# Fourier token transform on half its columns, rope tables on Pool, waits per norm tile, ropes beside qz

## What is computed

```python
def rms_norm(x, g):
    xf = x.astype(jnp.float32)
    y = xf * lax.rsqrt(jnp.mean(xf * xf, axis=-1, keepdims=True) + NORM_EPS)
    return (y * g.astype(jnp.float32)).astype(x.dtype)

def fourier_mix(h, w_in, w_out):
    b, n, _ = h.shape
    u, z = jnp.split(h @ w_in, 2, axis=-1)
    ug = u.reshape(b, n, FOURIER_GROUPS, D_BRANCH // FOURIER_GROUPS).astype(jnp.float32)
    mixed = jnp.fft.fft2(ug, axes=(1, 3), norm='ortho').real
    y = mixed.reshape(b, n, D_BRANCH).astype(h.dtype) * jax.nn.silu(z)
    return y @ w_out

def window_attention_mix(h, hc, w_in, sink, w_out, cos, sin, with_ctx_out):
    q, k, v, z = split_qkvz(h, w_in)
    qc, kc, vc, zc = split_qkvz(hc, w_in)
    q = apply_rope(q, cos, sin) * ATTN_SCALE
    k = apply_rope(k, cos, sin)
    ...
    out = (o * jax.nn.silu(z)) @ w_out
```

## Time and profile before

| | us |
|---|---|
| median of the runs | 3273.3 |
| lowest, highest | 3270.9, 3274.6 |
| profiled execution, its own time | 3273.4 |
| its span, first to last instruction | 3271.6 |
| PE busy | 3098.4 (95%) |
| DVE busy | 2398.7 (73%) |
| ACT busy | 1374.0 (42%) |
| POOL busy | 272.9 (8%) |

### The profile page before, as it was taken

How to read it: one execution, slowest core, us unless ns; L and a number is a source line. 1 busy time by engine, 2 the same in 40 slices (tenths; PEclk the granted TensorE clock), 3 DMA queues, 4 the chain that set the end, 5 groups by cost and what they waited for, 6 DMA issues and landing times.

```text
span 3271.6 us, 58750 instructions
## 1 busy us (share of the span) xinstructions
PE 3098.4 (95%) x24402; PEld 2958.1 (90%) x24402; DVE 2398.7 (73%) x3270; ACT 1374.0 (42%) x1470; POOL 272.9 (8%) x530
## 2 busy tenths in 40 slices
PE   5999989989999899999999999998999999899998
PEld 5997889989978799999999998996688999799998
DVE  6877888978778878865675667667867975567464
ACT  4335553443345534533433345334734333434332
POOL 0100000000000000000000110110000422000000
PEclk9999999999999999999999999999999999899999
DMA  5774456757745567665767674883156765377553
GB/s 206 278 281 170 173 172 244 275 209 279 270 167 174 201 246 255 210 237 193 256 234 257 230 267 167 295 295 142 59 215 229 225 199 189 135 263 248 194 216 129
DMA packets 130945, 710.37 MB, mean 217 GB/s; under 512 B 16392, under 2 KB 16544, under 8 KB 71584
## 3 DMA queue, kind: packets, MB, share of 16 engines
q1 hardware_dynamic: 67392, 484.47, 41.7%
q0 software_dynamic: 61264, 214.93, 18.6%
q10 hardware_dynamic: 2064, 7.70, 0.6%
HBM read 700.26 MB, written 2.10 MB: 215 GB/s over the span
## 4 chain that ended last, share of the span: by engine, by line
PE 82%; DVE 10%; ACT 4%; issue 3%; DMA 2%; ACTq 0%; DVEq 0%; POOLq 0%
PE bank L520 24%; PE bank L516 22%; PE bank L517 22%; PE bank L615 2%; DVE wlo L1594 2%; ACT whi L1044 2%; PE bank L865 1%; PE bank L844 1%; DMA aslab<-w_ada_dram 1%; DVE aslab L1619 1%; PE bank L567 1%; PE bank L625 1%; DVE sc L1713 1%; PE bank L952 1%; DVE xs L2205 1%
## 5 line engine op out<-in xcount | busy, mean ns | idle before, releaser
L516 PE MATMUL bank<-uhi,whi 128*128 128x256 f32 x6720 | 1662.0, 287 | 66.9 <-issue 35.1
L517 PE MATMUL bank<-ulo,whi 128*128 128x256 f32 x6720 | 1647.8, 285 | 0.0
L1044 ACT CAST whi<-raw 128x2048 fp32r<-128x2048 f32 (+1 forms) x464 | 876.0, 1889 | 1554.1 <-PE bank L520 1498.1
L1594 DVE TENSOR_TENSOR wlo<-raw,whi 128x2048 fp32r<-128x2048 f32 (+1 forms) x464 | 1053.4, 2271 | 614.4 <-ACT whi L1044 613.2
L516 PEld LDWEIGHTS bank<-uhi,whi 128*128 128x128 f32 x6720 | 1302.7, 194 | 76.6 <-issue 57.2
L517 PEld LDWEIGHTS bank<-ulo,whi 128*128 128x128 f32 x6720 | 1303.0, 194 | 1.2
L520 PE MATMUL bank<-uhi,wlo 128*128 128x256 f32 x6720 | 883.0, 284 | 5.5 <-DVE wlo L1594 5.5
L520 PEld LDWEIGHTS bank<-uhi,wlo 128*128 128x128 f32 x6720 | 838.6, 192 | 9.6 <-DVE wlo L1594 6.9
L460 POOL DMA_DIRECT2D aslab<-w_ada_dram x384 | 202.8, 528 | 2738.2 <-DVE mod L1619 1440.8
L1619 DVE CUSTOM_DVE_ANT_0 aslab<-aslab,sil,part 128x1024 f32<-128x1024 f32 x192 | 245.2, 1280 | 39.6 <-DMA aslab<-w_ada_dram 39.5
L1619 DVE CUSTOM_DVE_ANT_0 aslab<-aslab,sil,cols 128x1024 f32<-128x1024 f32 x192 | 245.1, 1280 | 35.4 <-DMA aslab<-w_ada_dram 35.4
(11 more groups left out here) (268 smaller groups left out, 2394.0 us busy)
## 6 DMA issues: line engine op xcount, KB each, us to landing
aslab<-w_ada_dram POOLq DMA_DIRECT2D x384, 512.0 KB, 5.0
raw<-w_win_dram SPq DMA_DIRECT2D x96, 1024.0 KB, 4.9
raw<-w_wfi_dram SPq DMA_DIRECT2D x96, 1024.0 KB, 5.3
raw<-w_wfo_dram SPq DMA_DIRECT2D x48, 1024.0 KB, 4.9
raw<-w_wci_dram SPq DMA_DIRECT2D x48, 1024.0 KB, 5.3
raw<-w_wo_dram SPq DMA_DIRECT2D x32, 1024.0 KB, 5.6
raw<-w_wpg_dram SPq DMA_DIRECT2D x32, 1024.0 KB, 5.3
raw<-w_wqz_dram SPq DMA_DIRECT2D x32, 1024.0 KB, 4.8
```

The lines of the kernel that those rows point to most:

```text
L516: nc.tensor.matmul(o, w_, xhi_, start=start, stop=False, skip_group_check=True)
L517: nc.tensor.matmul(o, w_, xlo_, start=False, stop=False, skip_group_check=True)
L1044: nc.scalar.copy(whi[:, s % 2, 0:n], raw[:, s, 0:n]).then_inc(s_hi, 1)
L1594: v.tensor_tensor(wlo[:, s, 0:n], raw[:, s, 0:n], whi[:, s % 2, 0:n].bitcast(F32), ALU.subtract).then_inc(s_lo, 1)
```

## The change

Four parts. The token transform computes columns 0 to 128 of the even and odd parts and `combine` writes the other 127 from the same columns read backwards, with the sign of the odd part turned. The rope table angles are computed on Pool, behind its first loads, with an operation more per step (Pool's multiply and add are two); ACT's Exp and Sin calls and DVE's lambda operations move inside run in0. In the first group of a run behind a norm PE waits for each tile of ulo instead of each four, and DVE's split of slab 1 moves from tile 5 of the norm to tile 8. The ropes of the second attention move behind the slabs of qz's last four groups on PE and beside their splits on DVE, and Silu of the gates into the drains.

```diff
+HALF = T // 2 + 1
@@ build @@
-        red = sb("red", 3 * T, at=place["trn"] + 3 * T * 4)
+        red = [sb(f"red{i}", 3 * T, at=place["trn"] + 3 * T * 4 * (i + 1)) for i in range(2)]
+        turns = sb("turns", 3 * T, at=place["trn"] + 3 * T * 4 * 3)
@@ gpsimd, behind load(0, 0), load(1, 1), wait for x, cond(0) @@
+            def follow(ins):
+                done[0] += 1
+                ins.then_inc(s_ang, 1)
+                pool.wait_ge(s_ang, done[0])
+            pool.wait_ge(s_in, 16 * INPUT_DMAS)
+            follow(nc.gpsimd.tensor_copy(ang[:, 0:T], posi[:, :]))
...
+            for i, (turn, back) in enumerate(((0.25, math.pi / 2), (0.0, 0.0))):
+                x = red[i][:, :]
+                follow(nc.gpsimd.tensor_scalar(trn[:, :], ang[:, :], 1 / TWO_PI, turn, ALU.mult, ALU.add))
+                follow(nc.gpsimd.tensor_scalar(trn[:, :], trn[:, :], ROUND, None, ALU.add))
+                follow(nc.gpsimd.tensor_scalar(trn[:, :], trn[:, :], -ROUND, None, ALU.add))
+                for c, y in ((C1, ang[:, :]), (C2, x), (C3, x)):
+                    follow(nc.gpsimd.tensor_scalar(turns[:, :], trn[:, :], -c, None, ALU.mult))
+                    follow(nc.gpsimd.tensor_tensor(x, turns[:, :], y, ALU.add))
+                follow(nc.gpsimd.tensor_scalar(x, x, back, PI32, ALU.add, ALU.min))
+                nc.gpsimd.tensor_scalar(x, x, -PI32, None, ALU.max).then_inc(s_sin, 1)
@@ tensor @@
-            def slab_t(s, par, lows):
+            def slab_t(s, par, lows, ready=None):
                 for k in range(4):
                     kt = 4 * s + k
+                    if ready is not None:
+                        pe.wait_ge(*ready(kt))
...
+                    if fill in NORMS and slab is slab_t:
+                        pe.wait_ge(s_hi, (g + r["m0"]) * SLABS + (s + 1))
+                        slab(s, par, False, lambda kt: (s_nl, 16 * U_NORMS[fill] + kt + 1))
...
-                            last = nc.tensor.matmul(bank[7][:, T * odd:T * (odd + 1)],
+                            last = nc.tensor.matmul(bank[7][:, T * odd:T * odd + HALF],
                                                     ab[:, g, t, P * odd:P * (odd + 1)],
-                                                    dft[:, t, T * odd:T * (odd + 1)],
+                                                    dft[:, t, T * odd:T * odd + HALF],
...
-            project("qz", None)
-            pe.wait_ge(s_drain, 2 * (RUN["qz"]["e0"] + 8))
-            for i in range(NJX):
-                rope(rope_jobs_x(), 2 * NJ, i)
+            project("qz", None, n=4)
+            def rope_behind(q):
+                if q == 2:
+                    pe.wait_ge(s_drain, 2 * (r["e0"] + 4))
+                if q < NJX:
+                    rope(rope_jobs_x(), 2 * NJ, q)
+            for g in range(4, 8):
+                group(r, g, (r["e0"] + g) % 2, slab_t, None, lambda s, g=g: rope_behind(4 * (g - 4) + s))
             pe.wait_ge(s_ro, 2 * NJ + NJX)
@@ scalar @@
+                    then=(f"v{l}",), hooks=((0, lambda: silu(2 * l)),)
+                    + (() if l else ((2, lambda_exps), (4, rope_tables))))
...
-                    nc.scalar.copy(evens[:, g % 2, :], bank[7][:, 0:T]).then_inc(s_fe, 1)
+                    nc.scalar.copy(evens[:, g % 2, 0:HALF], bank[7][:, 0:HALF]).then_inc(s_fe, 1)
...
-            act.wait_ge(s_drain, 2 * (RUN["qz"]["e0"] + 8))
-            nc.scalar.activation(zq_t[:, 16 * T:32 * T], zq_t[:, 16 * T:32 * T], ACT.Silu)\
-                .then_inc(s_gate, 1)
+            run(RUN["qz"], copier(zq_half), 0, 4, then=("qz", 4))
+            run(RUN["qz"], copier(zq_half, ACT.Silu), 4, 4)
@@ vector @@
-                    if kt == 5:
+                    if kt == 8:
                         split(RUN[AFTER_NORM[name]], 0, 1)
...
-                    v.tensor_tensor(zf[:, 2 * g, :], evens[:, g % 2, :], bank[7][:, T:2 * T], ALU.subtract)
-                    v.tensor_tensor(zf[0:P - 1, 2 * g + 1, :], evens[0:P - 1, g % 2, :],
-                                    bank[7][0:P - 1, T:2 * T], ALU.add).then_inc(s_fb, 1)
+                    even, odd = evens[:, g % 2, 0:HALF], bank[7][:, T:T + HALF]
+                    y, mirror = zf[:, 2 * g, :], zf[0:P - 1, 2 * g + 1, :]
+                    v.tensor_tensor(y[:, 0:HALF], even, odd, ALU.subtract)
+                    v.tensor_tensor(mirror[:, 0:HALF], even[0:P - 1, :], odd[0:P - 1, :], ALU.add)
+                    v.tensor_tensor(y[:, HALF:T], even[:, P - 1:0:-1], odd[:, P - 1:0:-1], ALU.add)
+                    v.tensor_tensor(mirror[:, HALF:T], even[0:P - 1, P - 1:0:-1], odd[0:P - 1, P - 1:0:-1],
+                                    ALU.subtract).then_inc(s_fb, 1)
...
-            run(RUN["qz"], nothing)
-            dve.wait_ge(s_drain, 2 * (RUN["qz"]["e0"] + 8))
+            run(r, nothing, 0, 4, then=("qz", 4))
+            def at_slab(q):
+                if q < 14:
+                    split(r, 4 + (q + 2) // 4, (q + 2) % 4)
+                ada(r, 16 + q)
+            ropes(rope_jobs_x(), 2 * NJ, table, 0, tuple((q, lambda q=q: at_slab(q)) for q in range(NJX)))
+            for q in range(NJX, 16):
+                at_slab(q)
+            dve.wait_ge(s_drain, 2 * (r["e0"] + 8))
```

More of the change, by code:

```diff
@@ L355, in build @@
         s_sin = sem("table_angle_ready")
+        s_ang = sem("table_steps")
         s_tab = sem("tables_ready")
@@ L473, in _ @@
             cond(0)
+            done = [0]
+            def follow(ins):
[4 more added lines that the diff above has]
+            follow(nc.gpsimd.tensor_copy(ang[:, 0:T], posi[:, :]))
+            for k in (2, 1, 0):
+                last = nc.gpsimd.tensor_scalar(ang[:, T * k:T * (k + 1)], ang[:, 0:T],
+                                               kk[:, K_INVF + k:K_INVF + k + 1], None, ALU.mult)
+            follow(last)
+            TWO_PI = 2 * math.pi
+            C1 = 6.28125
+            C2 = float(np.float32(np.round((TWO_PI - C1) * 2 ** 20) / 2 ** 20))
+            C3 = TWO_PI - C1 - C2
+            ROUND = 12582912.0
+            PI32 = 3.1415925
+            for i, (turn, back) in enumerate(((0.25, math.pi / 2), (0.0, 0.0))):
[8 more added lines that the diff above has]
+                nc.gpsimd.tensor_scalar(x, x, -PI32, None, ALU.max).then_inc(s_sin, 1)
             at = 2
@@ L1218, in silu, with lambda_exps, rope_tables @@
                 nc.scalar.activation(x, x, ACT.Silu).then_inc(s_sil, 1)
-            act.wait_ge(s_lam, 1)
-            act.dma_start(praw[:, :, :], vec["p"][0]).then_inc(s_p, 16)
-            nc.scalar.activation(sm[:, SM_TMP + 4:SM_TMP + 8], sm[:, SM_TMP:SM_TMP + 4], ACT.Exp)\
-                .then_inc(s_lam, 1)
-            for i in range(2):
-                act.wait_ge(s_sin, i + 1)
-                nc.scalar.activation(tabs[:, i::2, :], red[:, :].rearrange("p (k n) -> p k n", n=T),
-                                     ACT.Sin).then_inc(s_tab, 1)
+            def lambda_exps():
+                act.wait_ge(s_lam, 1)
+                act.dma_start(praw[:, :, :], vec["p"][0]).then_inc(s_p, 16)
+                nc.scalar.activation(sm[:, SM_TMP + 4:SM_TMP + 8], sm[:, SM_TMP:SM_TMP + 4], ACT.Exp)\
+                    .then_inc(s_lam, 1)
+            def rope_tables():
+                for i in range(2):
+                    act.wait_ge(s_sin, i + 1)
+                    nc.scalar.activation(tabs[:, i::2, :], red[i][:, :].rearrange("p (k n) -> p k n", n=T),
+                                         ACT.Sin).then_inc(s_tab, 1)
             def first_block(l):
@@ L1860, in _, with lambda_products @@
-            dve.wait_ge(s_tab, 2)
+            def lambda_products():
+                lv = lamr[:, :].rearrange("p (l q n) -> p l q n", l=2, q=4)
+                lp = sq[:, 0:256].rearrange("p (l q n) -> p l q n", l=2, q=2)
+                for l in range(2):
+                    last = v.tensor_tensor(lp[:, l], lv[:, l, 0:4:2], lv[:, l, 1:4:2], ALU.mult)
+                link(last)
+                v.tensor_reduce(sm[:, SM_TMP:SM_TMP + 4], sq[:, 0:256].rearrange("p (a n) -> p a n", n=64),
+                                AX.X, ALU.add).then_inc(s_lam, 1)
@@ new lines, in lambda_values @@
+            def lambda_values():
+                dve.wait_ge(s_lam, 2)
+                for l in range(2):
+                    a = SM_TMP + 4 + 2 * l
+                    link(v.tensor_tensor(sm[:, SM_LAM + l:SM_LAM + l + 1], sm[:, a + 1:a + 2], sm[:, a:a + 1],
+                                         ALU.subtract))
+                    v.tensor_scalar(sm[:, SM_LAM + l:SM_LAM + l + 1], sm[:, SM_LAM + l:SM_LAM + l + 1],
+                                    -LAM_INIT[l], None, ALU.add)
+                    link(v.tensor_scalar(sm[:, SM_SUBG + l:SM_SUBG + l + 1], col("subln_g", l),
+                                         1.0 - LAM_INIT[l], None, ALU.mult))
@@ L1881, in first_block @@
                 norm(f"n{l}")
-                run(RUN[f"in{l}"], nothing, then=(f"v{l}",))
+                run(RUN[f"in{l}"], nothing, then=(f"v{l}",),
```

(6 more changed lines are left out.)

60 lines of the change are left out of this document (9 added, 51 removed).

## The result

The median of the changed kernel is 3248.4 us (3247.7 to 3249.1, four runs), beside 3272.9 for the kernel before on the same chip: ratio 0.9928, 95% interval 0.9916 to 0.994. That is 24.5 us less where 44.2 were forecast, and outside the range of 3221 to 3242. The profiled execution's span is 3247.0, against 3271.6.

The account below looks back on a forecast made before the run. PE, busy 95% of the span, was taken as the bound. Gains 19.7 + 6.7 + 6.5 + 14.8 = 47.7, less 3.5 for Pool beside DVE, 44.2: 3273.4 - 44.2 = 3229.2 us, range 3221 to 3242.

Parts of the forecast that it names:

- The start (B): Program start: with the rope tables on Pool, the first whi begins at 18.3 instead of 25.01; 6.7 us earlier.
- C: Per-tile waits behind norms: first product earlier by 2.2 us at n0 and n1, 2.1 at nf3, nothing at nci; 6.5 us.
- Pool's chain: Rope tables on Pool, from 19.0 us: ending between 35.3 (DVE's durations) and 53 (twice the long ones), loads not held up.
- a rival priced at 4 us per operation: Rival 4: slow Pool arithmetic makes ada loads late, slower than before; 3295 us at 5 us each; chance 0.02.
- Turn-taking: Pool's arithmetic beside DVE in n0 delays the norm by 4.1 us, 0.6 of it free; cost 3.5 us.
- Rival 1: Pool and DVE take turns in full in n0, DVE 15 us late; gain 33.3 us, time 3240; chance 0.24.
- Late loads: First block: the third ada load, queued behind Pool's tables, goes out at about 57, not held up; no cost.
- A: Token transforms in three Fourier layers: 129 instead of 256 columns saves 0.82 us, 24 times; 19.7 us.
- Rivals 2 and 3: 2: weight loads bind the short transform products, 3244, chance 0.05. 3: DVE binds qz's second half, 3236, chance 0.08.
- D: Second attention's ropes moved into qz's second half: first score operation 13.8 us earlier, plus 1.0 for the clock; 14.8 us.
- Waits for late loads elsewhere: PE waiting for late condition-vector loads beyond the first block; the prediction had no term for it.

Follow-up runs that it names:

- spread_tables: Changed kernel with four long Pool table operations ahead, each other step behind one condition-vector load, ACT's Sin calls in in0's group 6, not 4; 3233.4 us, again 3231.9.
- no_tables: Changed kernel with the rope tables computed by DVE again, ahead of the program; token transform, per-tile waits and moved ropes stay; 3240.1 us, ratio 0.9906.
- first_table: Changed kernel with Pool computing the first table (cosines) in full and only one clamping operation for the second; 3240.0 us, ratio 0.9909.
- waits_only: Kernel before with only the per-tile waits of a norm's first slab and the second split behind tile 8; 3270.0 us, ratio 0.999, ten runs.
- second_after_norm: Changed kernel with one clamping operation for the first table, then Pool's full second table after the first norm, in front of the loads; 3242.8 us, ratio 0.9915.
- spread_defer: spread_tables with qz's last three condition-vector steps moved into the second attention, whose own steps go behind its fifth round; 3231.3 us, ratio 0.9885.

## Why the prediction was wrong

- **The start (B), 6.7.** The mechanism was right. The first whi came at 19.10, not 18.3, since ACT's table load of 1.28 us now stands in front of it. With most of Pool's work out of the way the first three slabs are 8.4 to 8.9 us ahead (spread_tables), against 8.9 for B and n0's part of C in the sum. Against no_tables, which has all but B, spread_tables is 6.6 us below in the medians (the intervals touch) and 5.6 by slabs at 480.
- **Pool's chain: the step that failed.** "The floor is DVE's own durations" and "The other end is twice that for the long ones", so a chain that ends between 35 and 53, and "Either end is before that, so the loads are not held up". Pool's operations took 2.13 us alone, 3.8 times DVE's, and 2.6 on average over all 22; the chain ended at 80.6. Twice DVE was no bound, only a guess in the form of one: no row had Pool's arithmetic, and then the other end has to be found by asking what length would hurt. I had that number, the third load out by about 60, a chain of 41 us, and gave it only to a rival priced at 4 us per operation with a chance of 0.02. That rival's mechanism is half of what happened; it needed 1.8 us per operation to begin. (The Trainium skill's figure, GPSIMD Engine Reference, Elementwise, made an estimate of 1.7 us for two sources; 1.80 to 2.05 were measured.)
- **Turn-taking, 3.5.** The Trainium skill's rule (SBUF — State Buffer, Who interferes with whom), that such a DVE instruction and a GpSimd instruction lock each other out for a whole one, agrees with this trace beside Pool's two-source operations: 0.41 against 2.03 us for one subtraction. Beside its one-source operations it does not hold for the whole of Pool's: 1.04 us, and DVE goes on at its usual pace while Pool's operation of 2.18 us still runs. The term was mis-sized: the norm was late by 6.8 instead of 4.1 us (two operations longer by 1.6 us, six by 0.6), and with the wait for slab 2's whi and the lower clock behind it PE lost 7.9 us (from -7.3 to +0.5). Rival 1 named this at 33.3 us for the whole change; first_table, which has this price and not the other, is 28.8 us below before.
- **Late loads, 0 in the sum.** Another 6.8 us from 61.5 to 90.3. Together the first 90 us give +7.3 where the sum had -5.4: 12.7 of the 19.7 us that are missing.
- **A, 19.7.** Right: 20.0. Rivals 2 and 3 did not happen; the reversed reads of the combine take 0.28 us like the forward ones, not twice as long.
- **C, 6.5.** n1's gap is 2.1 us shorter, as forecast; nci's gain is mostly given back, as forecast (0.5 remain in waits_only); nf3's was counted at 2.1 and keeps 0.9 in waits_only and 0.2 to 1.9 in the others, but for second_after_norm, which loses 1.6 there. I had looked for the next late thing one slab ahead only. The part alone is worth 1.2 us in time (0 to 6).
- **D, 14.8.** 13.8 by slabs in the changed kernel and 13.4 in the runs of the part alone. In the trace a condition-vector step that I did not list stands in front of the first score, behind a wait of 4.17 us; that it is the missing 1.0 us is not shown, since the runs could not tell the version that moves it (spread_defer, 0.6 us) from the one beside it.
- **Waits for late loads elsewhere**, 0 in the sum: some 7 us net in the changed kernel's profiled execution (between 90 and 2150 us, A and n1 taken out), 4 in its repetition, 2 in both traces of the spread version, and 4 to 8 in the traces of the other versions that have A and C together. The sum took the execution of before as if every other had the same waits. How much of this is chance is not settled, and what makes a load late at 626 in both traces of the changed kernel stays open.

The parts alone add up to about -26 (-20.6, -13.4, -1.2 and +9.1), against -24.5 measured together: within what the runs can tell, no dependence among them shows.

## What to carry to other kernels

Moving arithmetic to an idle engine is free only if its queue holds nothing else that is due: price the chain from a row of that engine, and where there is none, work out from which length it would hold up what is queued behind it, and give that case a real chance. The same work cost 13 us here in front of the loads and nothing that the runs can tell between them. A gap made shorter in front of a stage is only won if the engines that feed the following slabs get earlier too; follow it a group or two on, not one slab.

## What the runs showed of the hardware

- Pool needs 2.13 us for a one-source f32 operation on 128x768 where DVE needs 0.56, and 1.80 to 2.05 for a two-source one where DVE needs 0.96 for one that also multiplies. The operation with fewer sources is the slower one on Pool.
- Where the two take turns both pay: 4.06 to 4.70 us for Pool's operations instead of 2.13, 2.03 for DVE's instead of 0.41, 3.83 for a split instead of 2.28. The profile counts it all as busy. A two-source operation of Pool's held DVE's until its own end; a one-source one held it until 1.2 to 1.3 us from its start, and DVE worked beside the rest.
- A PE wait of 5 us cost 2.2 us more behind it: 7.99 us for a slab that began at the lower clock instead of 5.76.
- A product of 129 columns is not limited by the 190 ns that its weight load lasts in the trace: eight take 1.16 us, with the tail of the last, where eight times 190 ns would be 1.52.
- DVE reads 127 elements backwards from PSUM in 0.28 us, the same as forwards.
